# An encoder layer on one core: the first token tile of the last stage assembled from reads taken two experts early, plus one-hot products

## What is computed

```python
def hier_moe(h, w_group, b_group, w_erouter, b_erouter, w_gate_up, w_down):
    """Top-1 group, then top-2 experts within that group; gate = p_group * p_expert."""
    ...
    for e in range(N_EXPERTS):
        gu = t @ w_gate_up[e]
        y = (jax.nn.silu(gu[:, :D_EXPERT]) * gu[:, D_EXPERT:]) @ w_down[e]
        out = out + combine[:, e:e + 1] * y
    return out.reshape(B, S, D)

def encode(x, p, norm_mix, w_in, ...):
        ...
        x = x + jnp.concatenate([o_att, o_conv], axis=-1) @ w_out[i]
        h = rmsnorm(x, norm_ffn[i])
        x = x + hier_moe(h, w_group[i], b_group[i], w_erouter[i], b_erouter[i], w_gate_up[i], w_down[i])
        e = rmsnorm(p[i] @ w_ple_proj[i], ple_norm[i])
        x = x + jax.nn.sigmoid(x @ w_ple_gate[i]) * e
    return x
```

## Time and profile before

| | us |
|---|---|
| median of 3 runs | 639.3 |
| lowest, highest | 636.71, 639.71 |
| the profiled execution, whole | 639.58 |
| its span in the profile | 637.8 |

### The profile page before, as it was taken

The page is one execution under the profiler, slowest core; times in us unless marked ns, Lnnn a source line. Parts: engine busy times, 40 slices in busy tenths (PEclk is TensorE's granted clock), DMA queues, the critical chain, the costliest instruction groups (busy, mean ns, idle before and its releaser), DMA issues.

```text
span 637.8 us, 8493 instructions
## 1 busy us (share of the span) xinstructions
PE 611.7 (96%) x3080; PEld 497.7 (78%) x3080; DVE 407.0 (64%) x753; ACT 336.5 (53%) x605; POOL 62.9 (10%) x78
## 2 busy tenths in 40 slices
PE   5999999999999999999999999989999998699997
PEld 4878888888888777888888876768888887478885
DVE  6321356252642565656876988799999986756672
ACT  7741222231332675556554656799999986731211
POOL 0100000000000000100110124322221221010000
PEclk9999999999999999999999999999999999979999
DMA  8914305120221421213324758999999999533511
GB/s 352 376 25 177 99 2 186 32 76 33 67 67 66 174 85 48 96 38 104 124 83 170 238 195 343 392 361 414 412 405 400 389 402 372 208 122 116 178 38 66
DMA packets 36378, 120.03 MB, mean 188 GB/s; under 512 B 5576, under 2 KB 6216, under 8 KB 36336
## 3 DMA queue, kind: packets, MB, share of 16 engines
q1 hardware_dynamic: 30480, 106.29, 45.1%
q0 software_dynamic: 4896, 12.59, 5.1%
q10 hardware_dynamic: 960, 0.61, 0.3%
HBM read 106.84 MB, written 17.86 MB: 196 GB/s over the span
## 4 chain that ended last, share of the span: by engine, by line
PE 80%; DMA 8%; DVE 6%; ACT 3%; issue 2%; SPq 0%; ACTq 0%; POOLq 0%; DVEq 0%
PE bank L479 22%; PE bank L481 21%; PE bank L480 21%; PE bank L1792 6%; DMA w_raw_more<-in_w_moe 3%; PE bank L1819 3%; PE bank L1838 3%; DVE w_split L458 2%; PE bank L1800 2%; DMA p_raw<-in_pT 1%; DMA moe_rows<-moe_y,slot_row 1%; PE bank L1947 1%; ACT w_split L452 1%; ACT s L900 1%; DMA pick<-moe_rows 1%
## 5 line engine op out<-in xcount | busy, mean ns | idle before, releaser
L479 PE MATMUL bank<-w_split,h_T_prompt 128*128 128x512 f32 x192 | 77.6, 404 | 6.9 <-DVE w_split L1250 6.9
L481 PE MATMUL bank<-w_split,h_T_prompt 128*128 128x512 f32 x192 | 75.9, 395 | 0.0
L480 PE MATMUL bank<-w_split,h_T_prompt 128*128 128x512 f32 x192 | 75.8, 395 | 0.0
L474 DVE TENSOR_TENSOR w_split<-w_raw,w_split 128x1024 fp32r<-128x1024 f32 x33 | 40.2, 1221 | 41.5 <-ACT w_split L469 41.4
L479 PE MATMUL bank<-w_split,moe_xT 128*128 128x512 f32 x120 | 48.5, 404 | 2.2 <-DVE moe_xT L1639 2.2
L479 PEld LDWEIGHTS bank<-w_split,h_T_prompt 128*128 128x128 f32 x192 | 36.6, 191 | 15.1 <-DVE w_split L1250 6.9
L481 PE MATMUL bank<-w_split,moe_xT 128*128 128x512 f32 x120 | 47.0, 392 | 0.0
L480 PE MATMUL bank<-w_split,moe_xT 128*128 128x512 f32 x120 | 46.9, 391 | 0.0
L481 PEld LDWEIGHTS bank<-w_split,h_T_prompt 128*128 128x128 f32 x192 | 36.6, 191 | 7.9
L900 ACT ACTIVATE s<-s,mn 128x512 f32<-128x512 f32 (+1 forms) x48 | 30.9, 645 | 21.6 <-DVE mn L1311 21.6
L480 PEld LDWEIGHTS bank<-w_split,h_T_prompt 128*128 128x128 f32 x192 | 36.7, 191 | 7.2
(11 more groups left out here) (280 smaller groups left out, 1400.1 us busy)
## 6 DMA issues: line engine op xcount, KB each, us to landing
w_raw<-in_w_moe SPq DMA_DIRECT2D x32, 512.0 KB, 7.8
w_raw_room<-in_w_moe SPq DMA_DIRECT2D x30, 512.0 KB
w_raw_more<-in_w_moe SPq DMA_DIRECT2D x30, 512.0 KB
w_raw<-in_w_in SPq DMA_DIRECT2D x24, 512.0 KB, 5.4
pick<-moe_rows SPq DMA_DIRECT2D x10, 512.0 KB, 4.8
w_raw<-in_w_out SPq DMA_DIRECT2D x8, 512.0 KB, 3.4
toep<-bias_table SPq DMA_DIRECT2D x4, 896.0 KB, 7.2
x_row<-in_x SPq DMA_DIRECT2D x6, 512.0 KB, 9.2
```

Source lines behind the costliest of these rows:

```text
L474: nc.vector.tensor_tensor(W[:, u % WS, 1], raw(u)[0], f(W[:, u % WS, 0]), ALU.subtract).then_inc(lo_done, 1)
L479: nc.tensor.matmul(out, hi, whi, start=first, stop=False)
L480: nc.tensor.matmul(out, lo, whi, start=False, stop=False)
L481: return nc.tensor.matmul(out, hi, wlo, start=False, stop=last)
```

## The change

Six edits:
1. Tile 0 is read from `moe_rows` already when the scatter of expert t = 13 has landed, ahead of those of t = 14 and 15 (experts 13 and 14). So that rows not yet written count as zero, SP writes zeros there early in the kernel (two DMAs of 512 KB), and POOL's scatter of t = 14 waits until this early read has landed.
2. What experts 13 and 14 give to tile 0 is added by PE: DVE makes a one-hot matrix of each (the token's place in the expert's tile, times its routing weight; `late_hots`), PE turns them, ACT copies them (`late_hotT`), and `turn_first` sums, in float32 in PSUM, the early sum times the identity and the two experts' results times the one-hots: 12 products per half. `keep_clock` ahead of the stage goes.
3. Tile 0 is read a second time, in full, for the output's sum (the fourth pick, `PICKS`). The sums `x3` run two tiles ahead; tile 1 is turned in the middle of `gate(0, 1)`.
4. On SP, w_gate's units 4 to 7, five of the six residual reads and the load of `gain_row` (before: in the middle of the experts' loads) now stand behind the early read.
5. On ACT, the splits (16, 2) and (16, 3) stand behind `y_out(15)`, `x3T_hi(0)` is mixed with the splits 4 and 5, and all six `ple_square` stand ahead of `x3T_hi(1)`.
6. At t = 1 to 2, two splits, (3, 0) and (3, 1), stand ahead of a wait for PE instead of behind it.

```diff
@@ SP: 
             for u in STREAM:
-                if u == (8, 0):
-                    sp.dma_start(gain[:], gains[2]).then_inc(gain_ld, 16)
-                if u[0] > 5 or u in ((5, 4), (5, 5)):
+                if (u[0] > 5 or u in ((5, 4), (5, 5))) and u[0] <= LAST:
                     moe_unit(u)
+            for g in range(4):
+                moe_unit((LAST + 1, g))
...
-            for i in range(TILES):
-                x2_again(i)
+            x2_again(0)
+            sp.wait_ge(y_st[0], 16 * 6)
+            sp.wait_ge(y_st[1], 16 * 7)
+            sp.wait_ge(lp_done, 1)
+            sp.wait_ge(lo_done, MOE0 + AT[LAST - 1, 5] + 1)
+            for half in range(2):
+                pick_first(half)
+            for g in range(4, FIN_UNITS):
+                moe_unit((LAST + 1, g))
+            x2_again(1)
+            sp.wait_ge(d_hot, TILES)
+            sp.dma_start(gain[:], gains[2]).then_inc(gain_ld, 16)
             sp.wait_ge(y_st[0], 16 * 7)
             sp.wait_ge(y_st[1], 16 * 8)
-            sp.wait_ge(lp_done, 1)
-            for half in range(2):
-                pick_first(half)
             pick(1)
@@ POOL: scatters
                 pool.wait_ge(a_y, 2 * t)
+                if t == LAST - 1:
+                    for half in range(2):
+                        pool.wait_ge(part_ld[half], 48)
                 put(yb[t % 2], dst_u[:, t:t + 1], y_st[t % 2])
@@ ACT: early splits
             silu(1)
+            moe_hi((3, 0))
+            moe_hi((3, 1))
             act.wait_ge(pe_aT2, 1)
             act.activation(act_first[:], bank[3][:, 0:DE].rearrange("p (k t) -> p k t", k=2),
                            ACT.Copy).then_inc(a_aT2, 1)
-            for j in range(3):
-                moe_hi((3, j))
+            moe_hi((3, 2))
@@ ACT: last stage
+            act.wait_ge(pe_late, 1)
+            act.activation(late_hotT[:], bank[7][:, 0:2 * P].rearrange("p (e t) -> p e t", e=2),
+                           ACT.Copy).then_inc(a_late, 1)
+            actT_hi(LAST)
+            for g in range(2):
+                moe_hi((LAST + 1, g))
+            y_out(LAST)
+            for g in range(2, 4):
+                moe_hi((LAST + 1, g))
+            for half in range(2):
+                x3T_hi(0, (half,))
+                moe_hi((LAST + 1, 4 + half))
...
@@ DVE: last stage
+            x3_first(0)
+            actT_lo(LAST)
+            x3_first(1)
+            for g in range(4):
+                moe_lo((LAST + 1, g))
+            for half in range(2):
+                x3T_lo(0, (half,))
+                moe_lo((LAST + 1, 4 + half))
+            for g in range(6, FIN_UNITS):
+                moe_lo((LAST + 1, g))
+            x3(1)
+            x3T_lo(1)
+            x3(2)
             dve.wait_ge(gain_ld, 32)
@@ PE
+            def turn_first(half):
+                pe.wait_ge(d_x3, half + 1)
+                pe.wait_ge(a_late, 1)
+                pe.wait_ge(a_y, 2 * (LAST - 1))
+                out = bank[6 + half]
+                for q in range(4):
+                    k = slice((4 * half + q) * P, (4 * half + q + 1) * P)
+                    pe.matmul(out[:, tk(q)], ga[1][:, k], ident, start=(q == 0), stop=False)
+                    pe.matmul(out[:, tk(q)], yb[0][:, half, tk(q)], late_hotT[:, 0], start=False, stop=False)
+                pe.wait_ge(a_y, 2 * LAST - 1 + half)
+                for q in range(4):
+                    ins = pe.matmul(out[:, tk(q)], yb[1][:, half, tk(q)], late_hotT[:, 1],
+                                    start=False, stop=(q == 3))
+                ins.then_inc(pe_x3, 1)
...
-            keep_clock(36, bank[0][:], pTs[0][:, 0, 0:P], pTs[0][:, 0, 0:N])
-            turn_x3(0)
+            for half in range(2):
+                turn_first(half)
```

More of the change, by code:

```diff
@@ L1183, in _, with x3T_hi @@
                 y_out(t - 1)
-            actT_hi(LAST)
-            for g in range(4):
-                moe_hi((LAST + 1, g))
-            y_out(LAST)
-            for g in range(4, 6):
-                moe_hi((LAST + 1, g))
-            for g in range(6, FIN_UNITS):
-                moe_hi((LAST + 1, g))
-            def x3T_hi(i):
-                for half in range(2):
+            def x3T_hi(i, halves=(0, 1)):
+                for half in halves:
                     act.wait_ge(pe_x3, 2 * i + half + 1)
@@ L1741, in x3, with x3T_lo @@
                             ins.then_inc(d_x3, 1)
-            def x3T_lo(i):
-                for half in range(2):
+            def x3T_lo(i, halves=(0, 1)):
+                for half in halves:
                     dve.wait_ge(a_x3, 2 * i + half + 1)
@@ L2257 @@
         "late": late,
+        "zeros": np.zeros((P, D), np.float32),
     }
```

127 lines of the change are left out of this document (83 added, 44 removed).

## The result

The changed kernel takes 633.64 us (median of 6 runs, 631.63 to 634.19) against 639.29 us before (636.71 to 640.52): ratio 0.9911, 95% interval 0.9889 to 0.9934, so 5.7 us less, with 4.2 and 7.1 as the interval's ends. The profiled execution took 633.99 us, its span is 632.2. Predicted were 633.3 us. The number is right; several of its terms were not, and their errors nearly cancelled. One execution of the changed kernel was traced here, and another later (`after_again`); where they differ, the text says so.

A forecast was written before the change was run, and what follows sets the result against it. The prediction took the time to be decided by when `gate(1, 0)` can start, behind the last scatter and read back. 4.5 us at the end plus 1.8 further up, 6.3 off the profiled 639.58, gave 633.3 us; range 630.0 to 638.0.

The forecast's parts named there:

- The early read and what hangs on it: End of experts: tile 0's first sum at 542.4, `down(15)` 3.8 us later than before, taking 5.8 us at half clock.
- The early read is not queued behind w_gate: SP's queue about empty at the read, 0 to 1.5 us late; the opposite, 647.6 us, had chance 0.06.
- PE's wait at t = 3: Among the experts: PE's 1.69 us wait for DVE should go, as ACT's two splits move ahead of its wait.
- The landing of the last scatter: Scatter of t = 15, ahead of tile 1's read: taken to land after 7.06 us, at 558.6.
- The wait of 2 us for this sum inside `gate(0, 1)`: Sign of being right: PE waits about 2 us there for DVE's sum of tile 1.
- ACT's cover of half a us: ACT's splits, squares and copy ahead of `gate(1, 0)`: done at 569.9 against 570.4, the thinnest cover.
- rival A: PE stays at half clock through `turn_first`, so ACT's six squares become the bound: 637.4 us, chance 0.13.
- rival B: Clock falls again while PE waits for tile 1, price 2.2 us: 635.5 us; it and its like, chance 0.14.
- The upper part: Changes among the experts and earlier: 1.8 us gained, with bounds 0 and 3.0.
- half of the hole in DMA: Early splits free buffers sooner and can fill the hole (share 0.72 over 2 us), worth 0 to 1 us.
- The row's 1.3 us: Loading `gain_row` (512 KB) behind the experts' loads takes 1.3 us out of the full DMA stretch.
- the lost 1.3 us: Experts t = 11 to 14 took 29.28 us against three periods' 27.96; the loss was put down to DMA.

The follow-up runs named there:

- after_again: The changed kernel run and traced a second time, nothing changed: 632.27 us, ratio 0.9892 to the kernel before.
- gate_ahead: Changed kernel with w_gate's last four units (2 MB) issued ahead of the first residual block and early read: 635.98 us, ratio 0.9958 to before.
- b_splits: Kernel before with only ACT's two early splits of expert 3 put ahead of its wait for PE: 638.96 us, ratio 0.9997.
- best_clock: `best` with 12 unused matmuls added behind `down(15)`: 627.60 us, ratio 0.9826 to the kernel before.
- act_first: Changed kernel with DVE's low part of the last activations ahead of the first tile's sum: 629.86 us, ratio 0.9872 to before.
- act_first_squares: `act_first` plus tile 1's copy to x3T after three of ACT's six squares: 630.28 us, ratio 0.9861 to the kernel before.
- best2: `act_first_squares` plus two of w_gate's splits ahead of the first tile's sum on DVE: 632.02 us, ratio 0.9877 to before.
- best: `best2` with w_gate's last four units issued ahead of the early read: 627.92 us, ratio 0.9827 to the kernel before.

## Why the prediction was right, step by step

These steps were right:

- The early read and what hangs on it. The first sum starts 14.7 us behind silu of t = 14, 15.0 in the prediction (542.4 - 527.44). `down(15)` starts 3.45 us later than before, behind DVE's wait, 3.8 in the prediction (542.93 - 540.63 + 1.15). At half clock it takes 5.28 us, for 5.8.
- `turn_first` takes 5.33 us at full clock, 5.3 in the prediction, and the one-hots' small instructions are hidden.
- The early read is not queued behind w_gate, and PE's wait at t = 3 is gone.

These were wrong, by the terms of the sum:

1. **The landing of the last scatter**, taken at 7.06 from the earlier trace rows, was 4.1; with the read of tile 1 the sum started at 558.97 where the prediction, less 1.15, has 563.0. Of these 4 us the landing is 3. The step that failed is taking a duration from a row in which a backlog of loads lasted through most of the landing, for a moment at which the loads run out (DMA share 0.53 from 550 to 554, and 0.06 from 553 on); `gate_ahead` shows what the loads do to it. The wait of 2 us for this sum inside `gate(0, 1)`, which was to be the sign, is not there.
2. **ACT's cover of half a us.** The row of ACT itself was priced well (squares over at 565.73, predicted 566.4). With the sum 4 us sooner it was ACT that decided: rival A's bound, without its cause, the half clock in `turn_first`. The prediction names a wait of PE at `gate(1, 0)` for `x3T_lo(1)` as a sign of being wrong, and it is there, 1.99 us. `gate(1, 0)` could so start only 1.7 us sooner than predicted, not 4.
3. **The second fall of the clock**, rival B, took these 1.7 us back in the first trace (569 to 572). The prediction held against it that the fall before had needed 3.4 us of idle time; here it came behind a wait of 1.99 us. In the second trace it did not come, and that trace's tail is shorter by 6.4 us than before's instead of by 4.45.
4. **The upper part** is 0.7 us by the times and about 1.1 by the traces, not 1.8. The step that failed is half of the hole in DMA, given to the splits: `b_splits` shows the hole still there and no gain. The row's 1.3 us is 0.9 less 0.7 in single traces, 0.4 by the times with 0 in the interval. And the DMA share of 1.01 that the prediction reads for the lost 1.3 us is from 470 to 475, where the period is still 9.32; a full DMA by itself did not lengthen the period there.

So 633.3 came from 4.5 + 1.8; the changed kernel has 4.45 to 6.4 at the end, by the draw of the clock, and about 1 above. That the number is right is luck in part: at the end the sum of tile 1 came 4 us sooner than predicted, the squares took back 2.3 of them and the clock the rest. The direction rested on terms that held.

Three slips in the working changed little. The sum starts from the profiled execution (639.58 - 6.3 = 633.3); from the median of 639.3 it gives 633.0. From the last square to `gate(1, 0)` the prediction has 2.4 us in its row and 1.8 in rival A, and 1.95 were measured, so the cover was between half a us and one. And the little of rival A that lies under 636.1 adds to the chance of being faster, and was taken off it.

One rival stands untested. Before, the last scatter landed in 7.06 us beside a backlog of loads. Edit 4 alone, with the loads of w_gate and the residual out of its way, might have brought some 3 us of it (an estimate, 7.06 less the 4.1 measured here) without the early read and the one-hots. No run has the kernel before with that order of loads, so how the 4.45 to 6.4 us divide between edit 4 and the early read is open; `gate_ahead` shows only that the early read, once there, sets the end.

## What to carry to other kernels

The landing time of a small transfer belongs to what else the queues hold at that moment: take it from a row with the same load, and if none is at hand price both. Before pricing an instruction moved ahead of a wait in one engine's queue, look which engine is fed by what stands behind it: here two lines exchanged on DVE were worth 0.0020 to 0.0039 of the time, a fifth to nearly a half of what the change brought. Work that is ready sooner in front of a fixed arrival buys a longer wait, and on PE that wait can cost its clock as well; a few unused matmuls in it took that draw out in `best_clock`.

## What the runs showed of the hardware

The granted clock is a draw at the same program: in two traces of the changed kernel PE's last transpose ends at 538.4 and 538.1, and the first window with a fallen clock is that from 541 in the one and that from 543 in the other. Nor does the length of a wait decide: waits of 1.99 (changed kernel) and 1.97 us (`gate_ahead`) were followed by a fall, one of 1.73 (`after_again`) and those of 2.20 (`act_first`, `act_first_squares`) were not. It also fell in or right behind waits of 3.25 and 0.78 us (`best2`) and 3.04 us (`best`), and with the last one filled it did not. A scatter of 128 rows (512 KB) takes 3.2 to 4.7 us to land on queues that are empty or nearly so, and 6.7 to 8.0 beside loads (up to 10.3 early among the experts), even where the DMA share is only 0.50. With 512 KB of loads moved out of a full stretch, that stretch was 0.9 us shorter and another 0.7 longer, in one trace each, where traces of one program spread over 1.1 us.
